# MoE rows gathered on TensorE by selection matrices, with a third weight slot for the first 30 blocks

## What is computed

```python
def _hierarchical_moe(x, w_rg, b_rg, w_re, b_re, w_gate, w_up, w_down):
    ...
    g_w, g_idx = lax.top_k(jax.nn.softmax(g_logits, axis=-1), 1)
    e_w, e_idx = lax.top_k(jax.nn.softmax(e_logits, axis=-1), MOE_TOP_K)
    ...
    x_rows = jnp.concatenate([xf, jnp.zeros((1, d), x.dtype)], 0)[row_tok]
    x_rows = x_rows.reshape(n_blocks, MOE_BLOCK, d)

    def expert_block(args):
        xb, e = args
        h = jax.nn.silu(xb @ w_gate[e]) * (xb @ w_up[e])
        return h @ w_down[e]

    y_rows = lax.map(expert_block, (x_rows, block_e)).reshape(n_rows, d)
    y = jax.ops.segment_sum(y_rows * row_gate[:, None], row_tok, num_segments=t + 1)[:t]
...
    x = _layer_norm_2(DEEPNORM_ALPHA_2 * x + ffn, ln_g[i, 1], ln_b[i, 1])
```

## Time and profile before

| | us |
|---|---|
| median of 3 runs | 4502.24 |
| lowest and highest | 4499.92, 4510.23 |
| span of the profiled execution | 4483.4 |
| TensorE busy in it | 3907.5 |
| DVE, ACT, POOL busy | 1702.6, 701.0, 831.2 |
| DMA moved | 708.80 MB |

### The profile page before, as it was taken

The page is one execution under the profiler, slowest core; times in us unless marked ns, Lnnn a source line. Parts: engine busy times, 40 slices in busy tenths (PEclk is TensorE's granted clock), DMA queues, the critical chain, the costliest instruction groups (busy, mean ns, idle before and its releaser), DMA issues. The chain is left out here.

```text
span 4483.4 us, 62137 instructions
## 1 busy us (share of the span) xinstructions
PE 3907.5 (87%) x25636; PEld 2697.6 (60%) x25636; DVE 1702.6 (38%) x3092; ACT 701.0 (16%) x1502; POOL 831.2 (19%) x667
## 2 busy tenths in 40 slices
PE   7999989999999889999999996877749998677774
PEld 3578876784447777874448844444429976344442
DVE  6657757630465655221440613000033254200003
ACT  2212111110222221010211511000020033000000
POOL 1122214430110314420100202000013343100001
PEclk8999999999999999999999997989979999799997
DMA  3221313632121011232122025999962200899995
GB/s 134 66 95 49 124 44 131 219 129 99 48 66 57 2 53 59 92 108 66 49 75 68 1 85 223 398 400 402 401 237 67 85 1 34 329 401 394 404 401 227
DMA packets 253162, 708.80 MB, mean 158 GB/s; under 512 B 22441, under 2 KB 136689, under 8 KB 202253
## 3 DMA queue, kind: packets, MB, share of 16 engines
q1 hardware_dynamic: 234378, 660.87, 39.9%
q10 hardware_dynamic: 13956, 28.00, 1.7%
q0 software_dynamic: 4608, 16.78, 0.9%
HBM read 668.35 MB, written 37.24 MB: 157 GB/s over the span
## 5 line engine op out<-in xcount | busy, mean ns | idle before, releaser
L3374 PE MATMUL experts_pg<-moe_wg,experts_xt 128*64 128x256 f32 x4224 | 522.1, 410 | 132.8 <-DMA moe_wg<-in_moe_w_up 113.6
L3374 PEld LDWEIGHTS experts_pg<-moe_wg,experts_xt 128*64 128x64 f32 x4224 | 330.0, 148 | 307.9 <-issue 155.8
L3389 PE MATMUL experts_py<-moe_wd,experts_ht 128*64 128x512 f32 x1056 | 259.8, 636 | 41.6 <-DVE experts_ht L3444 24.1
L629 PE MATMUL ffn_out_y<-ffn_out_ring,ffn_h 128*128 128x512 f32 x640 | 275.9, 592 | 0.0
L3442 DVE TENSOR_TENSOR experts_h<-experts_hs,experts_pg 128x256 f32<-128x256 f32 x66 | 27.8, 421 | 642.4 <-ACT experts_hs L3408 642.4
L714 PE MATMUL ffn_in_seven<-ffn_in_seven_t,ffn_in_seven_s 128*128 128x256 f32 x1056 | 237.6, 381 | 1.7 <-DVE ffn_in_seven_t L787 0.8
L3474 POOL DMA_INDIRECT merge_yg<-y_rows,moe_yi x16 | 16.1, 1007 | 1103.8 <-PEq L3461 568.2
L714 PEld LDWEIGHTS ffn_in_seven<-ffn_in_seven_t,ffn_in_seven_s 128*128 128x128 f32 x1056 | 201.1, 191 | 31.6 <-DVE ffn_in_seven_t L787 1.6
L629 PEld LDWEIGHTS ffn_out_y<-ffn_out_ring,ffn_h 128*128 128x128 f32 x640 | 121.1, 190 | 151.6 <-issue 150.2
L3389 PEld LDWEIGHTS experts_py<-moe_wd,experts_ht 128*64 128x64 f32 x1056 | 82.7, 144 | 173.1 <-issue 173.1
L3438 DVE COPY experts_xt<-experts_px 128x512 f32<-128x512 f32 x66 | 45.6, 692 | 332.0 <-PE experts_px L3366 332.0
(11 more groups left out here) (755 smaller groups left out, 6814.9 us busy)
## 6 DMA issues: line engine op xcount, KB each, us to landing
moe_wg<-in_moe_w_gate SPq DMA_DIRECT2D x66, 2048.0 KB, 20.2
moe_wg<-in_moe_w_up SPq DMA_DIRECT2D x66, 2048.0 KB, 24.7
moe_wd<-in_moe_w_down SPq DMA_DIRECT2D x66, 2048.0 KB, 25.5
ffn_in_ring<-in_ffn_w_in SPq DMA_DIRECT2D x42, 1024.0 KB, 5.3
ffn_in_ada_ring<-in_ada_w SPq DMA_DIRECT2D x28, 1024.0 KB, 6.9
ffn_out_ring<-in_ffn_w_out SPq DMA_DIRECT2D x20, 1024.0 KB, 5.3
ssd_proj_ring<-in_ssd_w_in SPq DMA_DIRECT2D x19, 1024.0 KB, 5.4
att_kqt<-in_attn_w_qkv SPq DMA_DIRECT2D x17, 1024.0 KB, 5.1
```

The lines of the kernel that those rows point to most:

```text
L629: last = nc.tensor.matmul(y[:, tt, half, :], h[:, kk, tt * P:(tt + 1) * P], ring[n][:, q, half * BANK:(half + 1) * BANK], start=(kk == 0), ...
L3374: last = nc.tensor.matmul(pg[ch * SLOTS:(ch + 1) * SLOTS, b, side, 0:HH], xt[:, b, kk % MQ, kk // MQ, :], wg[:, b, side, kk, ch * HH:(ch + ...
L3389: last = nc.tensor.matmul(py[half * SLOTS:(half + 1) * SLOTS, b, :], ht[:, b, kk % HM, kk // HM, :], wd[:, b, kk, half * HALF:(half + 1) * ...
```

## The change

The rows of a block are no longer sent through HBM. For each pair of blocks (128 rows) DVE builds a selection matrix `sel`, 512 tokens by 128 rows, from the positions `yf` and an iota `seat`: two comparisons in one instruction, an add, and a shift of `yf` by -128 for the next pair. TensorE multiplies x_tok by it, which gives the transposed rows at once: 8 units of 4 matmuls, each unit one slice of 128 features. `xi`, `x_rows`, the scatter, the loads of `xg` and the transposes are gone. In the first 30 blocks the 8 units of the next pair are put between the steps of the present one: two ahead of a block's gate pass, one ahead of the transposes of h, one ahead of down.

Weights get a third slot: `up3` and `wd3` are new tiles, and its gate part lies in `ut`, which nobody reads after the logits. Blocks 0 to 29 are written out with slot n % 3 and their expert as a constant; blocks from 30 on run in a loop that uses slots 0 and 1 alone. Each of the three matrices of a slot has its own semaphore and is reloaded when its own pass is done. SiLU starts after the gate half. `py` has one bank instead of two. The counting is two matmuls of 128 columns, with the sums over earlier token tiles made by DVE. Several DVE steps that ran once per token tile now take all four. Blocks' experts and the pair count (`info`) are worked out in the expert stage. x_tok is not multiplied by ALPHA: the gates are divided by it, and the norm's epsilon by its square. The zero fill of x_rows early in the program goes.

```diff
+        spare = ExitStack()
+        up3, wd3 = (spare.enter_context(nc.sbuf_tensor(f"moe{l}_{n}", shape, F32)) for n, shape in (("up3", [P, DK, HID]), ("wd3", [P, HK, D])))
+        gate3 = k.ut[:, :, :].rearrange("p d t -> p (d t)")[:, 0:DK * HID].rearrange("p (k n) -> p k n", k=DK)
+        WSETS = 3
+        gate_in, up_in, down_in = ([outer.sem(f"{n}{b}") for b in range(WSETS)] for n in ("gate_in", "up_in", "down_in"))
...
+        def slot(n):
+
+            return n % 3, n // 3
+
+        def gate_up(w, side):
+            return wg[:, w, side, :, :] if w < 2 else (gate3, up3)[side]
+
+        def down(w):
+            return wd[:, w, :, :] if w < 2 else wd3[:, :, :]
...
-                    for b in range(2):
-                        load_gate_up(sp, slice(b, b + 1), b)
-                        load_down(sp, slice(b, b + 1), b)
+                    for n in range(2):
+                        w, _ = slot(n)
+                        load_gate(sp, one_of(n), w)
+                        load_up(sp, one_of(n), w)
+                        load_down(sp, one_of(n), w)
+                    load_up(sp, one_of(2), 2)
+                    load_down(sp, one_of(2), 2)
+                    sp.wait_ge(s["logits_made"], 1)
+                    load_gate(sp, one_of(2), 2)
...
+                    nc.tensor.matmul(pct[:, :, :], k.ones[:, :], m[:, :, :], start=True, stop=True).then_inc(s["counted"], 1)
+                    nc.tensor.matmul(prk[:, :, :], k.causal[:, 0, :], m[:, :, :], start=True, stop=True).then_inc(s["counted"], 1)
...
-                    pool.wait_ge(s["rows_done"], 1)
-                    for tt in range(TT):
-                        for j in range(2):
-                            nc.gpsimd.indirect_dma_start(out=x_rows[:, :], out_offset=bass.IndirectOffsetOnAxis(ap=xi[:, tt, j:j + 1], axis=0),
-                                                         in_=k.x[:, tt, :], in_offset=None).then_inc(s["sent"], 16)
-                    pool.wait_ge(s["sent"], 16 * 2 * TT)
...
-                    step(V.tensor_scalar(tmp[:, :], ew[:, :], 1.0, None, ALU.add))
+                    step(V.tensor_scalar(tmp[:, :], ew[:, :], 1.0, ALPHA, ALU.add, ALU.mult))
...
+                    step(V.tensor_tensor(pos[:, :, :], rank[:, :, :], late[:, :, :], ALU.add))
+                    for j in range(2):
+                        step(V.tensor_tensor(picked[:, j, :, :], pos[:, :, :], mj[:, j, :, :], ALU.mult))
+                    step(V.tensor_reduce(yf[:, :, :], picked[:, :, :, :], AX.X, ALU.add))
...
+                    def load(n, e, w, before):
+                        sp.wait_ge(s["gate_made"], before + 1)
+                        load_gate(sp, e, w)
+                        sp.wait_ge(s["gu_made"], before + 1)
+                        load_up(sp, e, w)
+                        sp.wait_ge(s["y_made"], before + 1)
+                        load_down(sp, e, w)
+
+                    for n in range(3, 2 * LAST):
+                        load(n, one_of(n), slot(n)[0], n - 3)
+                    end = pairs_end(sp)
+                    with sp.Fori(LAST, end) as it:
                         for b in range(2):
-                            load(2 * it + b, b)
+                            n = 2 * it + b
+                            e = sp.value_load(info[0:1, bass.ds(n, 1)], min_val=0, max_val=E - 1)
+                            load(n, bass.ds(e, 1), slot(2 * LAST + b)[0], n - 2)
...
-                        for m in range(MQ):
-                            last = nc.tensor.transpose(px[:, m, :], xg[:, b, m:HALF:MQ], k.ident[:, :])
-                        last.then_inc(s["xt_made"], 1)
...
+                    def unit(p, kk):
+                        q = p % 2
+                        for tt in range(TT):
+                            at = (kk // 4) * HALF + kk % 4
+                            last = nc.tensor.matmul(px[:, kk, :], k.x[:, tt, at:(kk // 4 + 1) * HALF:4], sel[:, q, tt, :],
+                                                    start=(tt == 0), stop=(tt == TT - 1))
+                        if kk % QUARTER == QUARTER - 1:
+                            last.then_inc(s["xt_made"], 1)
...
                         for side in range(2):
+                            pe.wait_ge((gate_in, up_in)[side][w], 16 * use + 16)
...
+                            last.then_inc(s[("gate_made", "gu_made")[side]], 1)
+                        if between is not None:
+                            unit(between, b * QUARTER + 2)
                         pe.wait_ge(s["h_done"], n + 1)
                         for m in range(HM):
                             last = nc.tensor.transpose(ph[:, m, :], h[:, b, m:HH:HM], k.ident[:, :])
                         last.then_inc(s["ht_made"], 1)
...
+                        if between is not None:
+                            unit(between, b * QUARTER + 3)
                         pe.wait_ge(s["ht_taken"], n + 1)
+                        pe.wait_ge(down_in[w], 16 * use + 16)
                         if not first:
-                            pe.wait_ge(s["y_taken"], n - 1)
+                            pe.wait_ge(s["y_taken"], n)
...
+                    for p in range(LAST):
+                        after = p + 1 if p + 1 < LAST else None
                         for b in range(2):
-                            one(2 * it + b, b, it)
+                            n = 2 * p + b
+                            if after is not None:
+                                begin(after, b)
+                                unit(after, b * QUARTER)
+                                unit(after, b * QUARTER + 1)
+                            if b == 0:
+                                pe.wait_ge(s["xt_taken"], 2 * p + 2)
+                            one(n, b, p % 2, *slot(n), after, n == 0)
+                    end = pairs_end(pe)
+                    with pe.Fori(LAST, end) as it:
+                        for half in range(2):
+                            pe.wait_ge(s["xt_taken"], 2 * it + half - 1)
+                            if half == 0:
+                                pe.wait_ge(s["sel_done"], it + 1)
+                            for kk in range(half * QUARTER, (half + 1) * QUARTER):
+                                unit(LAST, kk)
+                        pe.wait_ge(s["xt_taken"], 2 * it + 2)
+                        for b in range(2):
+                            w, use = slot(2 * LAST + b)
+                            one(2 * it + b, b, LAST % 2, w, it - LAST + use)
...
+                    def one(n, b, use):
+                        act.wait_ge(s["gate_made"], n + 1)
+                        if use is not None:
                             act.wait_ge(s["h_done"], n - 1)
...
-                    more = pairs_after_first(pool)
-                    for tt in range(TT):
-                        nc.gpsimd.tensor_scalar(k.x[:, tt, :], k.x[:, tt, :], ALPHA, None, ALU.mult).then_inc(s["x_scaled"], 1)
-                    pool.wait_ge(s["x_scaled"], TT)
+                    nc.gpsimd.iota(seat[:, :], pattern=[[1, P]], base=0, channel_multiplier=0,
...
+                    def select(p, q, first=False):
+
+                        if not first:
+                            dve.wait_ge(s["moved"], p)
+                            dve.wait_ge(s["sel_done"], p)
+                        V.tensor_tensor(hit[:, :, :, :], yf[:, :, :].unsqueeze(3).to_broadcast([P, 2, TT, P]),
+                                        seat[:, :].rearrange("p (j t n) -> p j t n", j=1, t=1).to_broadcast([P, 2, TT, P]),
+                                        ALU.is_equal).then_inc(s["hit_done"], 1)
+                        dve.wait_ge(s["hit_done"], p + 1)
+                        V.tensor_tensor(sel[:, q, :, :], hit[:, 0, :, :], hit[:, 1, :, :], ALU.add).then_inc(s["sel_done"], 1)
+                        V.tensor_scalar(yf[:, :, :], yf[:, :, :], -float(P), None, ALU.add).then_inc(s["moved"], 1)
+
+                    def take(p, half, q):
+                        dve.wait_ge(s["xt_made"], 2 * p + half + 1)
+                        V.tensor_copy(xt[:, q, half * QUARTER:(half + 1) * QUARTER, :], px[:, half * QUARTER:(half + 1) * QUARTER, :]).then_inc(s["xt_taken"], 1)
...
+                    for p in range(LAST):
+                        for b in range(2):
+                            one(2 * p + b, b)
+                            if p + 1 < LAST:
+                                take(p + 1, b, (p + 1) % 2)
+                            if b == 0 and p + 2 < LAST:
+                                dve.wait_ge(s["xt_made"], 2 * p + 2)
+                                select(p + 2, p % 2)
```

More of the change, by code:

```diff
@@ new lines, in _ @@
+                    dve.wait_ge(s["seat_done"], 1)
+                    step(V.tensor_copy(yi[:, :, :], yf[:, :, :].rearrange("p j t -> p t j")))
+                    select(0, 0, True)
+                    select(1, 1)
+                    for half in range(2):
+                        take(0, half, 0)
+                    blocks_beyond()
```

(13 more changed lines are left out.)

272 lines of the change are left out of this document (115 added, 157 removed).

## The result

The changed kernel takes 4592.62 us (median of four runs) beside 4502.24 us for the kernel before (median of three; a fourth run took 7839.38 us and is left out); the ratio on record is 1.0196, 95% interval 1.0173 to 1.0219. It is some 2% slower, where 4378 us, 3% faster, was forecast. The profiled span is 4592.5 us, 109 more than before.

A forecast was written before the change was run, and what follows sets the result against it. DMA bytes were taken to bound the MoE expert stages at 17.0 us a block. Gains of 60 and 64 us in the two layers take the span from 4483.4 to 4359.4; plus 18.8 gives 4378 us, range 4357 to 4430.

The forecast's parts named there:

- TensorE per block: Expert stages: a block with four gather units at 0.95 us each takes TensorE 15.1 us, bounds 14.7 to 16.3.
- The upper bound of 16.3 a block: TensorE's slowest expected block, with gather units no faster than the old gate/up share at mixed clock.
- The sign that the prediction named: Gather units in the expert stages taking over 1.1 us would show the forecast wrong.
- Rival (1): Expert stages: TensorE becomes the bound, slowed by its clock to 16.2 us a block; 4450 us, chance 0.17.
- the sum: Adds start, blocks and end per layer; layer 0 ends at 3244 us, layer 1 at 4363, gains 60 and 64.
- the 3 us for a crossing: Added per layer for a TensorE wait where its limit meets DMA's, with a 9.9 us pass replacing 7.13.
- 18.8 above the span, and that stays: Last step: the median was 4502.2 against a span of 4483.4 us; the same excess added to 4359.4 gives 4378.
- The waits for h and ht: Expert blocks: 0.9 and 0.6 us before, hidden under gather units; uncovered, 1.5 us a block would come back.
- The third slot: Weights load on before the first pass; if it did not help, both layers lose 31 us: 4409, chance 0.06.
- SP's ninth issue: Route stage: the last of nine early weight loads is issued near 2741.5 us, just under the cover of DVE.
- Bytes per block: Expert stages: without x row loads, a block's DMA time falls from 17.0 to 16.2 us.
- the lower bound of 15.65: Fastest expected DMA block: weights at the route stage's 422 GB/s plus 0.75 us for stores.

The follow-up runs named there:

- contiguous slices: Changed kernel with gather units reading 128 side-by-side x_tok elements instead of four words apart (feature order left wrong): 4344.91 us, ratio 0.9657 to the kernel before.

## Why the prediction was wrong, step by step

**The failed step** is "TensorE per block", and in it the price of a unit. It put 115 to 120 ns a record and 0.95 us a unit, by the attention projection and by the strided transposes; 240 ns a record and 2.0 us a unit were measured. The text saw the stride and excused it with a row of another operation: one record instead of two, and a group of four, in which 0.09 us are hard to see. So TensorE, put 1.1 us a block below DMA's 16.2, stood 2.5 above it and set the time of both stages. The upper bound of 16.3 a block allowed for a lower clock (the 9.92 us pass) and not for a slower record, so 18.72 lay above it. The sign that the prediction named, units over 1.1 us, is there. Rival (1), TensorE takes the bound, was the right place, but by a mechanism (the clock) that did not occur: the clock is 1.00 from the first gate/up pass on. With the measured block the sum closes. In each layer 28 blocks at 18.72 in place of 15.1, less the two units that already stand in the start (3.9), are 97.4 us more, 195 for both. The first passes come 7.0 and 5.0 us later after SP's first load than forecast, the blocks without units and the loop pairs take 6 and 13 more, and the 3 us for a crossing were not needed in either layer: 220 us together. With 10.9 us ahead of the stages and 2 elsewhere, 4359.4 becomes 4592.5.

The last step, from span to median, was wrong as well: "18.8 above the span, and that stays". The median of the changed kernel lies 0.1 above the span of its profile. Beside a miss of 215 us it does not matter here.

**What held.** yf 23.2 us after SP's first load (23.0 forecast). In the kernel with contiguous slices: units 0.93 us on average in a row (7.41 / 8), the first pass 2764.43 - 2726.54 = 37.9 us after SP's first load (38.5), a TensorE block of 14.84 (15.1). That the start of the stage's units fits so well, 10.99 us (10.9), is partly luck: the forecast had eight units and a wait for the take, and in the program ten units stand ahead of the first pass, without that wait. The waits for h and ht are covered, worth 67 us by the medians and 59 by the two stages. The third slot is worth 27 us (31). SP's ninth issue ends within the route stage with rows of 8 KB, 20.2 us after its first (20.7). Code: 15 packets in the changed kernel's 300 us from 2900, in which TensorE is busy throughout, so unrolling shows no cost.

**What was off in size.** Bytes per block: 16.2 was forecast, 15.56 measured, since the full rate without the x rows is 421 GB/s and not 401; the lower bound of 15.65, from the 422 GB/s of the route stage, was the better row. The x rows cost more than their bytes. With contiguous slices the change gains 155 us (4500.31 to 4344.91 on one chip), where 124 was forecast for the change as written. Of the 28 us by which its two expert stages are shorter than forecast, 19 are the blocks (56 x 0.26, and the two units a layer that stand in the start), 6 the crossings, and the rest small terms such as the blocks without units (12.2 for 12.5).

## What to carry to other kernels

Before a matmul reads an operand at a stride, look at the byte distance: 8 bytes were nearly free here on the stationary operand (the moving one was not tried), 16 bytes about doubled the matmul's time on either, and an order of the weights in memory or a copy off the path removes it. Price a new instruction by a row of the same operation and the same access, and long enough that the cost can be seen in it; a few short records beside waits prove nothing. When a change takes the second limit close to the first, put the measured slack of that second engine beside the error of its unit price: 1.1 us a block against 4 units was the whole forecast.

## What the runs showed of the hardware

- An fp32 128x128 weight load took 195, 200, 328 and 334 ns at steps of 1, 2, 4 and 8 words; a transpose's took 143 contiguous and 210 at 4.
- A moving operand at step 4 slowed the pair of records as much (3.91 us for 16), with weight loads at 207 ns.
- With gate and up weights in rows of 8, 4 and 2 KB (down always 8) DMA moved 421, 414 and 400 GB/s at a share of 1.02 to 1.04; two added 128 KB loads a block lowered 421 to 384.
- SP, issuing nine loads of 2.10 MB in the changed kernel, spent 0.4 to 2.1 us on each of the first six and 4.6 to 5.7 on each of the last three (2.10 MB at the 424 GB/s of 2750 to 2758 us are 5.0). With rows of 2 KB two issues took 8.6 and 8.7 us, and the next stage began only after the ninth.
- One 20 us stretch of unchanged code ran at a granted clock of 1.00, 0.77, 0.68 or 0.50 in the profiles of different kernels; SP's first load of the MoE stage stood at 2720.8 us in the first (before) and at 2731.6 in the last (changed).
